# A chain of fp32 layers on one Trainium2 core: the feed-forwards' first projections as seven half-size block products, their hidden tiles in two passes, and another order at the end of the convolution

## The reference

```python
def swiglu(h, w_gate, w_up, w_down):
    return (jax.nn.silu(h @ w_gate) * (h @ w_up)) @ w_down
...
    h = rmsnorm(x, ffn_norm[layer])
    x = x + swiglu(h, ffn_w_gate[layer], ffn_w_up[layer], ffn_w_down[layer])
```

```python
    a, gt = jnp.split(h @ w_pw1 + b_pw1, 2, axis=-1)
    z = a * jax.nn.sigmoid(gt)
    z = lax.conv_general_dilated(z, w_dw[:, None, :], ...) + b_dw
    z = jax.nn.silu(layernorm(z, ln_g, ln_b))
    return z @ w_pw2 + b_pw2
```

## Time and profile before

| | us |
|---|---|
| median of 3 runs | 1827.83 (1827.18 to 1831.11) |
| profiled execution, its device time | 1828.5 |
| its span in the profile | 1826.7 |
| PE busy | 1774.2 |
| DVE busy | 1030.1 |
| ACT busy | 661.2 |
| POOL busy | 184.4 |

### The profile page before, as it was taken

The page is one execution under the profiler, slowest core; times in us unless marked ns, Lnnn a source line. Parts: engine busy times, 40 slices in busy tenths (PEclk is TensorE's granted clock), DMA queues, the critical chain, the costliest instruction groups (busy, mean ns, idle before and its releaser), DMA issues.

```text
span 1826.7 us, 22495 instructions
## 1 busy us (share of the span) xinstructions
PE 1774.2 (97%) x8502; PEld 1433.2 (78%) x8502; DVE 1030.1 (56%) x1257; ACT 661.2 (36%) x768; POOL 184.4 (10%) x128
## 2 busy tenths in 40 slices
PE   7989999999999998899999999999999999999997
PEld 6767788888888765688888888888788888888876
DVE  7667564444444688664444444578856444444465
ACT  5328543333233322443333233342234333323342
POOL 1332100000000246100000000014600000000000
PEclk9899999999999999799999999999999999999998
DMA  6210233333233455133333233332213333323322
GB/s 212 78 46 1 70 92 92 92 104 102 68 97 96 117 147 144 59 96 104 92 92 96 82 96 95 105 86 70 70 61 85 108 92 92 93 85 107 95 86 75
DMA packets 284635, 168.12 MB, mean 92 GB/s; under 512 B 8288, under 2 KB 278528, under 8 KB 284576
## 3 DMA queue, kind: packets, MB, share of 16 engines
q1 hardware_dynamic: 283952, 165.64, 32.2%
q0 software_dynamic: 624, 1.67, 0.3%
HBM read 156.59 MB, written 2.10 MB: 87 GB/s over the span
## 4 chain that ended last, share of the span: by engine, by line
PE 93%; DVE 4%; issue 1%; ACT 1%; DMA 1%; SPq 0%; POOL 0%; DVEq 0%; ACTq 0%; POOLq 0%
PE ps L862 28%; PE ps L864 28%; PE ps L863 28%; PE ps L1192 2%; PE ps L1057 1%; PE ps L1100 1%; PE ps L1082 1%; DMA raw<-in_nsa_w_in_dram 1%; PE ps L1112 0%; PE ps L1300 0%; DVE wlo L1411 0%; DVE act_lo L1441 0%; DVE sqacc L1431 0%; PE ps L934 0%; DVE qkd L1944 0%
## 5 line engine op out<-in xcount | busy, mean ns | idle before, releaser
L862 PE MATMUL ps<-act_hi,whi 128*128 128x512 f32 x1756 | 693.2, 395 | 17.4 <-DVE act_lo L1443 8.7
L863 PE MATMUL ps<-act_lo,whi 128*128 128x512 f32 x1756 | 686.9, 391 | 0.0
L864 PE MATMUL ps<-act_hi,wlo 128*128 128x512 f32 x1756 | 686.7, 391 | 0.0
L1411 DVE TENSOR_TENSOR wlo<-raw,whi 128x2048 fp32r<-128x2048 f32 (+1 forms) x156 | 357.3, 2290 | 183.7 <-ACT whi L542 183.3
L862 PEld LDWEIGHTS ps<-act_hi,whi 128*128 128x128 f32 x1756 | 331.8, 189 | 99.2 <-issue 24.8
L863 PEld LDWEIGHTS ps<-act_lo,whi 128*128 128x128 f32 x1756 | 331.9, 189 | 69.4 <-issue 1.2
L864 PEld LDWEIGHTS ps<-act_hi,wlo 128*128 128x128 f32 x1756 | 331.7, 189 | 69.5
L542 ACT ACTIVATE whi<-raw 128x2048 fp32r<-128x2048 f32 (+1 forms) x164 | 306.6, 1870 | 197.1 <-PE ps L864 185.8
L1425 DVE TENSOR_TENSOR t<-ps,rstd 128x512 f32<-128x512 f32 x151 | 103.6, 688 | 266.0 <-PE ps L864 265.1
L862 PE MATMUL ps<-hid_hi,whi 128*128 128x512 f32 x528 | 208.0, 394 | 0.0
L864 PE MATMUL ps<-hid_hi,wlo 128*128 128x512 f32 x528 | 207.0, 392 | 0.0
(11 more groups left out here) (346 smaller groups left out, 1323.3 us busy)
## 6 DMA issues: line engine op xcount, KB each, us to landing
raw<-in_ffn_w_gate_dram SPq DMA_DIRECT2D x44, 512.0 KB, 3.9
raw<-in_ffn_w_up_dram SPq DMA_DIRECT2D x44, 512.0 KB, 5.1
raw<-in_w_gate_upffn_dram SPq DMA_DIRECT2D x44, 512.0 KB, 4.5
raw<-in_ffn_w_down_dram SPq DMA_DIRECT2D x32, 384.0 KB, 3.7
raw<-in_conv_w_pw_dram SPq DMA_DIRECT2D x24, 512.0 KB, 5.6
raw<-in_w_in_dram SPq DMA_DIRECT2D x24, 512.0 KB, 4.4
raw<-in_ffn_w_down_dram SPq DMA_DIRECT2D x32, 320.0 KB, 4.1
z<-z SPq DMA_DIRECT2D x28, 262.0 KB, 4.9
```

Of the source, the lines that this page charges most:

```text
L862: pe.matmul(out, lhs[0], rhs[0], start=start, stop=False)
L863: pe.matmul(out, lhs[0], rhs[1], start=False, stop=False)
L864: return pe.matmul(out, lhs[1], rhs[0], start=False, stop=stop)
L1411: ve.tensor_tensor(wlo[:, n % 2, a], raw[:, n % 2, a], whi[:, n % 2, a].bitcast(F32), ALU.subtract)\
```

## The change

Three things are changed.

**1. Seven block products for each hidden tile.** The gate and the up weights of a hidden tile are taken as one matrix of two column blocks (gate, up), and cut in two along the 1024 channels: four weight blocks of 512 channels by 128. The activations are cut the same way, in channels (0 to 511, 512 to 1023) and in tokens (0 to 255, 256 to 511). A 2x2 by 2x2 block product is then done with seven block products in place of eight (the form of Strassen's method with 15 additions). A block product is 4 x 3 = 12 matmuls of 256 columns, so a hidden tile takes 84 matmuls of 256 columns instead of 48 of 512. The names of the products in the code are B11, B21, T2, T1, T3, B22 and T4. T4 of a tile is issued after B11 of the next (`fourth`).

- Weight side: `weight_sums` on GpSimd makes four sums of 128x512 for each hidden tile (`w_sums`), two in place in `raw`, two in `ssum`. The splitting of three more blocks goes to ScalarE (`hi_sum`) and VectorE (`lo_sum`, L1917 of the changed kernel).
- Activation side: `late` makes the combinations `g12`, `n1`, `tt2`, `tt3`, `tt4` and their high and low parts (`bt_hi`, `bt_lo`, and `act_hi`, `act_lo` for T1, T3, B22, T4).
- Result side: ScalarE copies three partial results out of PSUM (`take`), VectorE adds the others (L1994, L2000, L2006) and multiplies by the reciprocal norm (L2007, L2011, L2013). The rest (silu, L2017, `hid_hi`, `hid_lo` in L2022) is as before.

**2. Two passes.** `hid_hi` and `hid_lo` have room for 12 hidden tiles. The feed-forward runs 12 hidden tiles, a down projection over these, 10 hidden tiles, and a down projection over these. Each down projection adds its eight tiles to `x`. The loops over hidden tiles and output tiles are written out.

**3. End of the convolution.** `convolve(m-3)` runs ahead of panel m, so three convolutions stand after the last panel. The last tile's shifted copies are issued half by SyncE and half by ScalarE. VectorE's `combine` comes one step later. In the layer norm the mean is spread in two steps with `repeat_rstd` between them, and VectorE's reciprocal comes ahead of its subtractions.

```diff
 def ffn(f, q, up, down):                       # TensorE
...
+    def fourth(u, n):
+        pe.wait_ge(sem("up_summed"), 3 * u + 1)
+        product(up_banks(dn, u)[0], plain(n, 3), "T4", False, panel_done, u == KF * f)
+
+    for k in ks:
+        u, n = KF * f + k, N0[up_] + k - ks[0]
+        a, b, c = up_banks(dn, u)
+        first = k == 0
+        pe.wait_ge(sem("up_split"), 3 * u + 1)
...
+        product(a, plain(n, 0), "B11", True, sem("up_product"), first)
+        if k > ks[0]:
+            fourth(u - 1, n - 1)
+        product(c, plain(n, 1), "B21", True, sem("up_product"), first)
+        pe.wait_ge(sem("up_split"), 3 * u + 2)
+        pe.wait_ge(sem("taken"), 3 * u + 1)
+        product(a, summed(0), "T2", False, sem("up_product"), first)
+        product(b, plain(n, 2), "T1", True, sem("up_product"), first)
+        if first:
+            sumsq(q)
+        pe.wait_ge(sem("up_split"), 3 * u + 3)
+        pe.wait_ge(sem("taken"), 3 * u + 2)
+        product(a, summed(1), "T3", False, sem("up_product"), first)
+        pe.wait_ge(split_done, n + 1)
+        pe.wait_ge(sem("taken"), 3 * u + 3)
+        product(b, summed(2), "B22", False, sem("up_product"), first)
+    fourth(u, n)
...
 def weight_sums(f, up_):                       # GpSimd, new
...
+    r = raw[:, n % 2].rearrange("p (c t) -> p c t", c=4)
+    pool.wait_ge(raw_full[n % 2], 32 * ((n + 1) // 2))
+    pool.tensor_tensor(r[:, 2], r[:, 2], r[:, 3], ALU.add).then_inc(sem("w_sums"), 1)
+    pool.wait_ge(sem("w_sums"), 4 * u + 1)
+    if u:
+        pool.wait_ge(sem("up_split"), 3 * u - 1)
+    pool.tensor_tensor(ssum[:, 0], r[:, 2], r[:, 0], ALU.subtract).then_inc(sem("w_sums"), 1)
+    pool.wait_ge(sem("w_sums"), 4 * u + 2)
+    if u:
+        pool.wait_ge(sem("up_split"), 3 * u)
+    pool.tensor_tensor(ssum[:, 1], r[:, 3], ssum[:, 0], ALU.subtract).then_inc(sem("w_sums"), 1)
+    pool.wait_ge(sem("up_split"), 3 * u + 1)
+    pool.tensor_tensor(r[:, 1], r[:, 1], ssum[:, 0], ALU.subtract).then_inc(sem("w_sums"), 1)
...
 def take(u, dn, i):                            # ScalarE, new
+    act.wait_ge(sem("up_product"), 6 * u + (1, 3, 4)[i])
+    dst = (t1[:, u % 2, 0:HALF], t1[:, u % 2, HALF:], t2[:, u % 2, HALF:])[i]
+    act.activation(dst, (a, a, b)[i][:, 0:HALF], ACT.Copy).then_inc(sem("taken"), 1)
...
 # ScalarE, for each hidden tile
+    hi_sum(u, n, 2)
+    take(u, dn, 0)
+    if k > ks[0]:
+        silu(u - 1)
+    if k < ks[-1]:
+        hi_panel(u + 1, n + 1)
...
+    if k > ks[0]:
+        cast_hidden(u - 1)
+    take(u, dn, 1)
+    if k < ks[-1]:
+        hi_sum(u + 1, n + 1, 0)
+    take(u, dn, 2)
...
 # convolution, TensorE
-for m in range(2, KD):
-    convolve(m - 2)
+panel2("pw1", 2)
+for m in range(3, KD):
+    convolve(m - 3)
     panel2("pw1", m)
...
-convolve(KD - 2)
-convolve(KD - 1)
+for m in range(KD - 3, KD):
+    convolve(m)
...
 # convolution, SyncE and ScalarE
-for i in range(NS):
+for i in range(NS if m < KD - 1 else NS // 2):
...
+    for i in range(NS // 2, NS):
+        act.dma_start(z4[:, b, i, 0:width], shifted(b, i, width)).then_inc(sem(f"z_stacked{b}"), 16)
```

More of the change, by code:

```diff
@@ L36 @@
 KF = FH // P
-KHALF = KF // 2
+PARTS = (range(0, 12), range(12, KF))
+HALF = S // 2
+Q4 = KD // 2
 IN1 = 1816
@@ L675, in _ @@
             cast_output(3)
[L677 to L686, removed]
-                        act.wait_ge(bank_free, T0[name] + k + 5)
-                        if k == KD - 1:
-                            act.wait_ge(panel_done, N0[name] + 4)
-                            cast(act_hi[:, k], x[:, k], f"xhi{q}", gain(q, k))
-                        square(q, k, x[:, k])
@@ L693, in _, with hi_panel @@
[L693 to L717 removed]
+            def hi_panel(u, n):
+                act.wait_ge(sem("w_sums"), 4 * u + 1)
+                act.wait_ge(panel_done, n - 1)
+                act.activation(whi[:, n % 2], raw[:, n % 2], ACT.Copy).then_inc(hi_done, 1)
@@ new lines, in hi_sum, with take @@
+            def hi_sum(u, n, c):
+                act.wait_ge(sem("w_sums"), 4 * u + 2 + c)
+                if u:
+                    act.wait_ge(sem("up_product"), 6 * (u - 1) + (3, 5, 6)[c])
+                act.activation(sw_hi[:, c], ssum[:, c] if c < 2 else raw[:, n % 2, Q4 * P:2 * Q4 * P], ACT.Copy)\
+                    .then_inc(sem("sum_hi"), 1)
+            def take(u, dn, i):
+                a, b, _ = up_banks(dn, u)
+                if i == 0 and u >= 2:
+                    act.wait_ge(sem("hidden_lo"), u - 1)
+                act.wait_ge(sem("up_product"), 6 * u + (1, 3, 4)[i])
+                dst = (t1[:, u % 2, 0:HALF], t1[:, u % 2, HALF:], t2[:, u % 2, HALF:])[i]
+                act.activation(dst, (a, a, b)[i][:, 0:HALF], ACT.Copy).then_inc(sem("taken"), 1)
@@ L1154, in _, with plain @@
             last_panel("mix")
[L1156 to L1172 removed]
+            def plain(n, c):
+                return lambda k: slot(n, c * Q4 + k, P)
@@ L1221, in _, with spread_mean @@
             pe.wait_ge(sem("ln_dve"), 1)
-            for out in (ps[4], bank(T0["pw1"] + 12)):
+            def spread_mean(out):
                 for b in range(TB):
@@ new lines, in lo_panel, with lo_sum @@
+            def lo_panel(u, n):
+                ve.wait_ge(hi_done, n + 1)
+                ve.tensor_tensor(wlo[:, n % 2], raw[:, n % 2], whi[:, n % 2].bitcast(F32), ALU.subtract)\
+                    .then_inc(sem("up_split"), 1)
+            def lo_sum(u, n, c):
+                ve.wait_ge(sem("sum_hi"), 3 * u + 1 + c)
+                src = ssum[:, c] if c < 2 else raw[:, n % 2, Q4 * P:2 * Q4 * P]
+                ve.tensor_tensor(sw_lo[:, c], src, sw_hi[:, c].bitcast(F32), ALU.subtract)\
+                    .then_inc(sem("up_split") if c < 2 else split_done, 1)
```

473 lines of the change are left out of this document (328 added, 145 removed).

## The result

The changed kernel takes 1881.5 us (median of 4 runs, 1880.66 to 1882.38), the kernel before 1829.23 (4 runs). The ratio is 1.0286, 95% interval 1.0271 to 1.0302: **slower by 2.9%**. The profiled run took 1880.66 us, its span is 1878.9.

What follows compares the result with a forecast made beforehand. TensorE bound the kernel before; VectorE, taking turns with GpSimd, would bound the changed tiles. From the profiled 1828.5 us, three feed-forwards add 51 and the convolution's end takes 10: 1869.5, stated as 1869 us; range 1793 to 1907.

Steps and rivals of the forecast that it cites:

- Taking turns: Feed-forwards: a VectorE pass with two SBUF operands and a GpSimd sum don't run at once; 7.57 + 5.08 = 12.65 us a tile.
- A steady tile: Feed-forward's hidden tile: 12.65 us less 0.56 and 0.68 leaves 11.4 us, with VectorE as the bound.
- Start of a feed-forward: After the mixer's last matmul, x[:, 7] starts at 7.1 us, B21's last quarter comes at 9.0, T2 at 12.6.
- First projections: Each feed-forward's hidden tiles: 145.9 us for the first pass of 12, 109.9 for the second of 10.
- Down projections: The two in each feed-forward have the columns of the one before, so together they stay at 120.8 us.
- End of the convolution: Reordered last panel, copies and layer norm save 10 us; bounds -5 and -13.
- The wait: TensorE's 6.81 us ahead of the last convolution gives back 5.9 us and falls under 2 us.
- the rest: End of the convolution beyond the wait: 4 us, from the last 40 matmuls at full clock and the layer norm's order.
- The first: Feed-forwards: GpSimd's sums don't hold VectorE up; tile 10.08 us, feed-forward 351, kernel 1788; chance 0.15.
- All PSUM passes hidden: Feed-forward tiles: all four VectorE passes that read PSUM run beside sums; 10.7 us a tile, kernel 1831; chance 0.12.
- sums as cheap as 1.06: GpSimd's weight sums take 1.06 us each instead of 1.27; 48 us less, kernel 1821; chance 0.08.
- the fourth: Chain through ScalarE closes worse, 12.1 us a tile, or the clock falls in tiles' waits: +38, 1907; chance 0.13.

Runs made afterwards that it cites:

- Experiment 1: Changed kernel with each GpSimd weight sum replaced by three writes of a constant to the same target, reading nothing: 1791.8 us.
- experiment 8: Changed kernel with three of a tile's four weight sums moved to VectorE, only the fourth left on GpSimd: 1842.22 us, ratio 1.0083.
- Experiment 5: Changed kernel with all sums on VectorE and another order ahead of each feed-forward, x[:, 7] added ahead of the lows of T1, T3, B22: 1816.53 us.
- experiment 3: Kernel before with only the end of the convolution changed: 1819.33 us, ratio 0.9956.
- 6: Experiment 5's kernel with hid_lo 49152 bytes behind hid_hi in place of 24576: 1816.39 us.
- 10: Experiment 5's kernel with TensorE's down projections in loops again: 1816.97 us.
- 11: Experiment 5's kernel with hid_lo 36864 bytes behind hid_hi in place of 24576: 1816.43 us.
- 9: Kernel before with TensorE's loop over the down projection's output tiles written out: 1826.9 us, ratio 0.9995.

## Why the prediction was right, and where its terms were off

It said 1869 us, slower; 1881.5 was measured, inside the range. The change was 52 us where 41 was forecast. Of the 11 between them, 7 are the down projections, 3.5 the first projections and 3.7 the convolution; the other stretches took 3.2 less, so a part of the closeness is luck.

- **Taking turns: shown.** Experiment 1 takes the reading away and makes GpSimd's steps longer, and the tile falls from 11.47 to 9.96; experiment 8 puts one sum back and the tile rises by the 0.5 us worked out.
- **A steady tile, 11.4: measured 11.47.** The matmuls of 256 columns are 0.117 to 0.120 apart, 9.96 a tile in experiment 1, where 0.120 and 10.08 were taken.
- **Start of a feed-forward, 7.1, 9.0 and 12.6 us: measured 7.3, 9.1 and 12.7.** Experiment 5 adds what the prediction had wrong in its picture: it told the hole as one of queue order (`x[:, 7]` behind lows). With that order changed, the hole moved and 0.5 us of 136.4 came back. By that, VectorE's amount of work sets the time here.
- **First projections, 145.9 and 109.9: measured 147.4 and 110.6**, where 1.5 more had been put aside for the clock. The granted clock did fall, to 0.83 in 246.5 to 276 us, where before it was 1.00. FFN3's first 12 tiles took 149.1, 1.6 more than the others; no run asked why.
- **Down projections, 120.8: measured 123.2.** This is the term that failed: "the two down projections have the columns of the one before" is true, but each matmul takes 0.2333 instead of 0.2289. In three feed-forwards that makes 7 us of the 11 by which the change was larger than forecast. The prediction put nothing on it and gave no reason; what makes the spacing larger stays open (see the last section).
- **End of the convolution, -10: measured -6.3** (-7.4 alone, in experiment 3), inside the bounds. Two terms were mis-sized. The wait was priced at 5.9 us and gave 3.9; it should have been under 2 us and was 2.89. The copies for tile 7 go into the buffer that convolution 5 reads, and wait until it is done. Convolution 5 now stands behind the last panel. `z` is there at 739.41, but the copies are issued at 740.84, right behind the end of convolution 5 at 740.73. I had let them come with the panel. The split gave 1.1 us of 2.1. The other term, 4 us for the rest, gave 2.4. That term had the last convolution's 40 matmuls fall from 6.45 us to 4.5 at full clock, but they took 7.08: the granted clock over them was 0.63 (748.4 to 755.5), lower than the 0.68 of before (733.5 to 739.9). The 0.78 shown above is the mean of a longer stretch.
- **Rivals.** The first, 1788 with 351 us a feed-forward, is nearly what experiment 1 gives once the sums don't read (1791.8, and 351.9 to 352.4): its price was right and its condition false. "All PSUM passes hidden" (10.7) and "sums as cheap as 1.06" (10.6) are ruled out by the tile of 11.47; so is the fourth, 12.1, and the granted clock was 1.00 in 300 to 380 us.
- The other stretches gave back 3.2 us together; nothing shows that this is more than the difference from run to run.

The fastest version run, 1816.4 to 1817.0 us in experiments 5, 6, 10 and 11, is faster than both kernels, but little of that is the seven products'. Its interval overlaps with that of the convolution's part alone (0.9956, 0.9942 to 0.9970). The profiles can tell more: in all four runs each feed-forward takes 359.8 to 360.1 us, 361.1 or 361.2 with the products of before, so the seven products with all sums on VectorE are worth 3 to 4 us of the whole.

## What to carry to other kernels

A half-idle engine isn't a free one. Ask of a helper's instruction not how long it runs but whom it stops: here 5 us of GpSimd a tile looked free beside 7.6 us of VectorE, and the two added up to a bound above TensorE's. When multiplications are saved by additions, count the additions' passes on the engine that splits and scales (twelve or sixteen a tile here, five before) against the saving (0.9 us a tile), and when an order of work is moved, look for the buffer whose reader moved with it.

## What the runs showed of the hardware that was not expected

- GpSimd's plain writes (128x512, 0.53 us each) ran beside VectorE's passes with two SBUF operands, which kept their 0.68; sums that read did not. The Trainium skill, "SBUF — State Buffer", section "Who interferes with whom", says so of an instruction that only writes, and experiment 1 agrees.
- Where the two take turns, GpSimd's sum shows as 1.62 to 1.68 us and VectorE's pass as 1.33 to 1.80: each record has the wait in it. Neither tells its cost by itself; the period of the tile does. The turns are not strict, either: at the start of FFN1 the sum L440 is recorded from 248.28 for 3.58 us, and two VectorE passes (of 1.22 and 0.95 us, begun at 248.66 and 249.79) went ahead of it. What decides the turn, no run shows.
- 128x512 matmuls on the hidden tiles are 0.2333 us apart in two passes of 12 and 10, 0.2289 (0.226, 0.229 and 0.232 in turn) in halves of 11, and 0.2267 on `act_hi`. It isn't the loop (9, 10), nor the distance of `hid_hi` and `hid_lo` (24576, 36864, 49152 bytes: all 0.2333); 64 bytes of shift changed the pattern, to 0.2324 on the mean. The places of the weights, 1536 and 1280 columns a panel instead of 1408, were not tried; the cause stays open.
